# Products on TensorE that nothing reads, ahead of and behind the norms' statistic

## The reference

```python
def rms(x):
    xf = x.astype(jnp.float32)
    return (xf * lax.rsqrt(jnp.mean(xf * xf, axis=-1, keepdims=True) + EPS)).astype(x.dtype)
def modulate(x, shift, scale):
    return rms(x) * (1 + scale[:, None]) + shift[:, None]
```

## Time and profile before

| | us |
|---|---|
| timed executions, median (lowest to highest) | 2438.36 (2435.56 to 2440.43) |
| profiled execution, its own time | 2450.89 |
| its span, first to last instruction | 2449.2 |
| TensorE busy in it | 2302.3 (94%) |
| VectorE busy in it | 1341.4 (55%) |
| ScalarE busy in it | 954.4 (39%) |
| mean granted clock of TensorE | 0.974 of full speed |

### The profile page before, as it was taken

One profiled execution on the slowest core, in us unless ns is written; L12 is line 12 of the kernel. 1 busy time (PEld: TensorE's weight loads), 2 busy tenths in 40 slices (PEclk: granted clock), 3 DMA queues, 4 the chain that ended last, 5 costly groups with the idle time before them and its releaser, 6 DMA issues.

```text
span 2449.2 us, 34895 instructions
## 1 busy us (share of the span) xinstructions
PE 2302.3 (94%) x12802; PEld 1905.8 (78%) x12802; DVE 1341.4 (55%) x1880; ACT 954.4 (39%) x1383; POOL 166.1 (7%) x170
## 2 busy tenths in 40 slices
PE   5999998999999979999999979899999997999999
PEld 5778766788888868888888866686778885888887
DVE  6465466566667455525534555646745564645544
ACT  3454556422223253213312335545643343533333
POOL 2123010000000000000000001310100000000000
PEclk9999999999999989999999989899999998999999
DMA  7111110234343311121111131120135542222223
GB/s 275 43 52 53 51 39 19 78 131 145 129 146 120 112 43 60 60 69 61 60 60 62 59 131 43 61 70 26 48 104 178 174 164 102 86 94 95 98 97 114
DMA packets 58621, 221.21 MB, mean 90 GB/s; under 512 B 6720, under 2 KB 6720, under 8 KB 57872
## 3 DMA queue, kind: packets, MB, share of 16 engines
q1 hardware_dynamic: 44496, 160.46, 19.4%
q0 software_dynamic: 14016, 59.26, 7.0%
HBM read 214.45 MB, written 5.24 MB: 90 GB/s over the span
## 4 chain that ended last, share of the span: by engine, by line
PE 86%; DVE 5%; ACT 4%; issue 3%; DMA 2%; DVEq 0%; SPq 0%; ACTq 0%
PE PS L577 83%; PE PS L830 3%; ACT TM L982 2%; DMA RA<-w_ada 1%; ACT XY L982 1%; DVE XY L1293 1%; DVE F_lo L1290 1%; ACT W_hi L982 1%; ACT F_hi L982 1%; DVE TM L1293 1%; DVE W_lo L1290 0%; DMA XY<-x_in 0%; DMA XY<-x_spill 0%; ACT H_hi L982 0%; DVE XY L1499 0%
## 5 line engine op out<-in xcount | busy, mean ns | idle before, releaser
L1290 DVE TENSOR_TENSOR W_lo<-W_st,W_hi 128x1024 fp32r<-128x1024 f32 x278 | 341.7, 1230 | 775.9 <-ACT W_hi L982 758.6
L577 PE MATMUL PS<-H_hi,W_hi 128*128 128x512 f32 x2240 | 686.0, 363 | 57.2 <-DVE H_lo L1290 38.7
L577 PE MATMUL PS<-H_hi,W_lo 128*128 128x512 f32 x2240 | 674.7, 358 | 0.0
L577 PE MATMUL PS<-H_lo,W_hi 128*128 128x512 f32 x2240 | 671.3, 357 | 0.0
L982 ACT ACTIVATE W_hi<-W_st 128x1024 fp32r<-128x1024 f32 x278 | 293.7, 1057 | 877.0 <-PE PS L577 867.4
L577 PEld LDWEIGHTS PS<-H_hi,W_hi 128*128 128x128 f32 x2240 | 374.1, 191 | 136.5 <-issue 64.1
L577 PEld LDWEIGHTS PS<-H_lo,W_hi 128*128 128x128 f32 x2240 | 370.7, 191 | 65.2 <-issue 1.5
L577 PEld LDWEIGHTS PS<-H_hi,W_lo 128*128 128x128 f32 x2240 | 369.6, 190 | 62.1
L577 PE MATMUL PS<-F_hi,W_hi 128*128 128x512 f32 (+1 forms) x952 | 290.8, 360 | 17.3 <-DVE XY L1293 6.4
L577 PE MATMUL PS<-F_lo,W_hi 128*128 128x512 f32 (+1 forms) x952 | 288.3, 357 | 0.0
L577 PE MATMUL PS<-F_hi,W_lo 128*128 128x512 f32 (+1 forms) x952 | 287.8, 357 | 0.0
(11 more groups left out here) (130 smaller groups left out, 2098.2 us busy)
## 6 DMA issues: line engine op xcount, KB each, us to landing
W_st<-w_all SPq DMA_DIRECT2D x278, 512.0 KB, 3.4
RA<-w_mod POOLq DMA_DIRECT2D x40, 512.0 KB, 3.6
TM<-w_mod POOLq DMA_DIRECT2D x40, 512.0 KB, 3.7
RA<-w_ada SPq DMA_DIRECT2D x8, 512.0 KB, 8.6
XY<-bias_na POOLq DMA_DIRECT2D x2, 1792.0 KB, 8.0
RA<-w_mod SPq DMA_DIRECT2D x6, 512.0 KB, 8.0
XY<-x_in SPq DMA_DIRECT2D x4, 768.0 KB, 11.3
x_spill<-XY POOLq DMA_DIRECT2D x1, 3072.0 KB, 10.4
```

Source lines behind the costliest of these rows:

```text
L577: return nc.tensor.matmul(o, lhsT, rhs, start=start, stop=stop)
L1290: return nc.vector.tensor_tensor(o, a, b, f)
```

## The change

Where a norm makes its own statistic (the last three of the four), TensorE first runs four products, identity by four of the constant matrices, 128x512 in plain float32, into bank 4; they stand behind the wait for the phases of ScalarE and VectorE (L642) and ahead of the wait for the sum (L635). In all four norms it then waits for `y0`, the reciprocal root, and runs w // 128 + 1 more such products, 7 in the wide norms and 5 in the narrow one, before it ends its phase and comes to `two_early_tiles`. Nothing reads bank 4 until real products have written it anew. The other engines' programs are unchanged.

```diff
+            def spin(n):
+
+                for _ in range(n):
+                    mm(bank(4), MT[:, M_ID, :], MT[:, 0:4, :].rearrange("p a n -> p (a n)"), True, True)
+
-            def squares_of_x(w):
+            def squares_of_x(w, n=0):
+                spin(n)
                 pe.wait_ge(S["sq_sum"], base["sq_sum"] + KT - 1)
                 for s0, sn in segs(w):
                     ins = mm(pair(3)[:, s0:s0 + sn], MT[:, M_ONE, :], TT[:, s0:s0 + sn], True, True)
...
             def norm(ph, w, summed=False):
                 if not summed:
                     begin(pe, ph, "act", "dve")
-                    squares_of_x(w)
+                    squares_of_x(w, 4)
+                pe.wait_ge(S["y0"], base["y0"] + 1)
+                spin(w // P + 1)
                 base.advance(sq_sum=KT - 1)
                 base.advance(**norm_counts())
```

## The result

| | before | changed |
|---|---|---|
| timed, median of 7 | 2438.36 | 2452.15 |
| lowest to highest | 2433.63 to 2445.29 | 2449.86 to 2458.74 |
| profiled execution, span | 2449.2 | 2448.8 |

The ratio is 1.0053, 95% interval 1.0035 to 1.0072: the changed kernel is slower, by 13.8 us by the medians and 12.9 us (8.5 to 17.6) by the ratio; 13.0 were forecast. The two profiled executions are nearly equal in length.

What follows compares the result with a forecast made beforehand. TensorE, busy 94% of the span, and its few waits were taken to set the end. 2 x (5.5 - 1.3) + (5.5 - 0.9) = 13.0 us, the rest 0, gave 2438.36 + 13.0 = 2451.4 us; range 2446.5 to 2460.

Steps and rivals of the forecast that it cites:

- The four products do not fall into the idle time: Before the statistic in three norms: the idling precedes VectorE's release, so every microsecond of the four products is on the path.
- Their price: Four products ahead of the statistic: 5.5 us per norm, 4.9 to 5.9 by clock bursts, outer bounds 3.4 and 6.8.
- when the clock comes back: In the four products, begun cold: full clock returns after 4.2 us, mean of four bursts; bounds 3.05 and 4.99 us.
- What the statistic gives back: The statistic's product then runs at 2.4 GHz, saving 1.3 us in each wide norm and 0.9 us in the narrow one.
- The products behind the root are free, and bring nothing: Seven or five products while TensorE awaits `H_lo`: hidden, gain 0, bounds -0.5 to 0 us per norm.
- the slack at 3.0 us: First real products behind the root: they may start 3.0 us late at no cost, 2.1 us in the narrow norm.
- before each of the steps 1 to 3: Expected sign in the early tiles: TensorE waits for `H_lo` before each of these steps, longer than before.
- with full clock from the first unit step 3 and what follows run as before: Early tiles: step 3 still begins when `H_lo[3]` is there, and the 13 units behind it were fast already; gain 0.
- cold time is lost time: Rival for the norms: half of each cold stretch is lost, so the change is faster, 2425 us; chance 0.06.
- Identity times constants: Rival: these products do not bring the clock up, costing 34 us in all, 2472 us; chance 0.06.
- A delay swallowed whole: Rival: something fixed in time, such as POOL's spill of x, hides the delays; all three hidden gives 2438; chance 0.05.
- named signs of being wrong: Four products beginning before the last sum ends, steps 3 to 10 ending sooner after `H_lo[7]`, or shorter stages behind the norms.

## Why the prediction was right

*The four products do not fall into the idle time.* Right: they begin 0.20 us behind the last sum, the wait ahead of them is as long as before, and the run with these four alone has the whole cost. The run in the idle time shows it from the other side: six such products a few lines earlier cost nothing.

*Their price.* 5.5 us for four were forecast, 4.9 to 5.9 by the bounds of the clock; the profile has 5.24, 6.56 and 6.24, mean 6.0. The term was 0.5 us too small, and two of three lie above the bound. The step behind it, when the clock comes back: the stretch of 6.48 us has a mean grant of 0.53 and that of 6.15 us one of 0.55, so the level rose only near their ends, about 6 us and 5.5 us after the first product. The five bursts of the earlier trace rows had come to 5 us at most; five were too few to be bounds. All three lie inside the outer bounds, 3.4 and 6.8 us, and those had made the range.

*What the statistic gives back.* Forecast 1.3 and 0.9 us; measured 1.45 (2.90 to 1.45) and 1.03 (2.05 to 1.02), by the records. The two errors go against each other: 18.0 us for the products less 3.9 us for the statistic are 14.1, against the 13.0 forecast and the 13.8 of the medians. That 13.0 lies within 1 us of what was timed is in part luck, since the interval is 9 us wide.

*The products behind the root are free, and bring nothing.* Right in both halves. They ended late in two of the norms seen above (the first real product 0.34 and 0.38 us behind them, with `H_lo[0]` ready before). In the second norm the grant was still 1.00 when they began and fell 1.5 us later, with the engine busy (0.50 from 873.65 to 876.80, 0.79 over the seven). It cost nothing; the run with these products alone shows no change in time, and twice as many measure the slack at 3.0 us, the figure of the forecast. The warm start bought only longer waits for `H_lo`. These did not come before each of the steps 1 to 3, as had been foretold, but only in the narrow norm: in the second TensorE came late to step 1, and in the third the clock was down at step 2. One sentence of this step did fail: that with full clock from the first unit step 3 and what follows run as before. In the second norm of the run with the products behind the root alone, the clock fell once more in step 2, after two waits, and step 3 began at 1.2 GHz, 0.8 us lost where 0 had been put as the worst; no time of a whole run could tell it.

*The rivals.* That cold time is lost time is refuted for the real products: with the products behind the root alone they start warm, and the step that matters does not come sooner. For the statistic the rule holds, since there TensorE is what the others wait for: half of 2.90 us came back. This is what the forecast had set against the rule of the Trainium skill that half of the throttled time is lost, "TensorE: Matmul & The Clock Gate", section "HAM oscillation"; the trace agrees with it only where TensorE's product is itself on the path. Identity times constants did not leave the clock down: the grant is 1.00 at the statistic behind the products. A delay swallowed whole is excluded by the times; some of it swallowed is not, with 14.1 us added in the norms and 8.5 to 17.6 timed. One of the named signs of being wrong did appear, for in the two profiles stages behind the norms got shorter; the last section says what is known of that.

## What to carry to other kernels

A product run only to hold the clock must stand in time in which the engine idles anyway. Between the last sum and the statistic, on the path, it was paid in full, and at 1.2 GHz double; ahead of the wait for the phases it was free, and behind the root it was free up to a slack of 3.0 us. Before cold time is bought back, ask at each cold stretch what the next step waits for: where another engine released the products one by one (steps 0 to 2 here), their clock had no value. Then look at what else stands in that chain: here taking an activation's table load of 1.28 us off it, four times, brought 6.3 us (2.7 to 10.2) by one line.

## What had not been expected of the hardware

The same products ran at one of two paces, both at a grant of 1.00. In the stretch from 600 to 700 us TensorE is busy throughout, with products of the merge. Here it is for the kernel before and then for the changed one; the second figure is TensorE's busy time and its products:

```profile
600.00:700.00 100.00, 100.00 (x568) 86.80 (x567) 62.72 (x87) 25.52 (x29) 7.39 (x14) 1.00 0.40 133
```
```profile
600.00:700.00 100.00, 100.00 (x578) 88.15 (x578) 63.87 (x88) 26.90 (x30) 7.40 (x14) 1.00 0.41 137
```

Over all ten profiles this stretch has 567 to 569 products in five and 578 or 579 in the other five, and nothing between. It does not go with the edit: the two profiles of the kernel with idle-time products and early table, the same program, have 567 and 578. It is not fixed for an execution either: from 1100 to 1200 us the changed kernel has 568, as the kernel before has 567, while the second of those two still has 579. What chooses the pace was not found.

This is one part of why the two spans are equal, and it can be dated. The last sum of the second norm ends at 868.21 before and at 862.88 in the changed kernel, 5.3 us earlier, ahead of the first of the four products. The change's only part ahead of it is the seven products of the first norm, behind which step 3 is 0.58 us later (62.50 for 61.92), just as the statistic there was (43.63 for 43.05). From there to the third norm's last step ahead of the statistic (1452.54 and 1447.31) the changed kernel takes 0.1 us more although its second norm grew by 3.8; from the third to the fourth (2068.01 and 2062.35) 0.4 us less although 5.2 were added; from the fourth to the end 5.3 us more, just what was added. So 5.3, 3.7 and 5.6 us came back from elsewhere, 14.6 in all, against 14.2 in the norms. The pace accounts for some of it: ten products in 568 are 1.8 us in each 100. How much of the rest is the clock's falling at other moments was not separated. Single executions of the kernel before lie 12 us apart, so a comparison of two profiles has to go place by place.
